# Another order of loads, splits and normalisations in the opening of a two-layer streaming encoder step

## What is computed

```python
c_kv = rmsnorm(kv_lat, lp['mla_kv_norm'])
k_rope = apply_rope(kr_raw, pos)
lat_all = jnp.concatenate([past[0], c_kv], axis=1)      # 512 cached latents of 256, then the new ones
kr_all = jnp.concatenate([past[1], k_rope], axis=1)
kv = (lat_all @ w_kvup).reshape(B, K, MLA_HEADS, MLA_NOPE_DIM + MLA_V_DIM)
k_nope, v = kv[..., :MLA_NOPE_DIM], kv[..., MLA_NOPE_DIM:]
k = rmsnorm(jnp.concatenate([k_nope, kr], axis=-1), qk_k_norm)
```

## Time and profile before

| what | value |
|---|---|
| median of 3 runs | 1045.93 us (1045.85 to 1046.44) |
| profiled execution, its own time | 1047.23 us |
| its span, first to last instruction | 1045.3 us |
| mean granted TensorE clock | 0.998 |
| TensorE busy | 1038.8 us of the span |
| TensorE's share of the chain that ended last | 97% |
| memory read | 142.11 MB, 139 GB/s over the span |

### The profile page before, as it was taken

The page is one execution under the profiler, slowest core; times in us unless marked ns, Lnnn a source line. Parts: engine busy times, 40 slices in busy tenths (PEclk is TensorE's granted clock), DMA queues, the critical chain, the costliest instruction groups (busy, mean ns, idle before and its releaser), DMA issues.

```text
span 1045.3 us, 20059 instructions
## 1 busy us (share of the span) xinstructions
PE 1038.8 (99%) x7586; PEld 1005.6 (96%) x7586; DVE 641.6 (61%) x1079; ACT 506.8 (48%) x930; POOL 314.3 (30%) x277
## 2 busy tenths in 40 slices
PE   8999999999999999999999999999999999999998
PEld 6899999999999999999998999999999999999998
DVE  6888764445766666543567886554557565565443
ACT  6557755444554444434355585554445444433341
POOL 3365566541221111100133755656312211111000
PEclk9999999999999999999999999999999999999999
DMA  7455533244535544454514544333344354444441
GB/s 243 118 157 124 185 103 120 90 133 142 161 120 164 159 146 155 142 180 145 178 45 137 149 145 135 96 119 122 120 154 152 124 177 141 154 147 146 156 145 67
DMA packets 48707, 146.29 MB, mean 140 GB/s; under 512 B 8800, under 2 KB 14400, under 8 KB 48640
## 3 DMA queue, kind: packets, MB, share of 16 engines
q1 hardware_dynamic: 42416, 143.05, 44.3%
q10 hardware_dynamic: 6224, 2.30, 0.9%
HBM read 142.11 MB, written 3.22 MB: 139 GB/s over the span
## 4 chain that ended last, share of the span: by engine, by line
PE 97%; DVE 2%; DMA 0%; ACT 0%; issue 0%; SPq 0%; ACTq 0%
PE psum L566 29%; PE psum L567 28%; PE psum L568 28%; PE psum L739 1%; PE psum L778 1%; PE psum L761 1%; PE psum L721 1%; PE psum L722 1%; PE psum L726 1%; PE psum L769 1%; PE psum L698 1%; PE psum L811 1%; PE psum L994 0%; PE psum L866 0%; PE psum L693 0%; PE psum L694 0%
## 5 line engine op out<-in xcount | busy, mean ns | idle before, releaser
L566 PE MATMUL psum<-AH,WH 128*128 128x320 f32 x1328 | 414.4, 312 | 0.2
L568 PE MATMUL psum<-AH,WL 128*128 128x320 f32 x1328 | 410.3, 309 | 0.0
L567 PE MATMUL psum<-AL,WH 128*128 128x320 f32 x1328 | 410.2, 309 | 0.0
L566 PEld LDWEIGHTS psum<-AH,WH 128*128 128x128 f32 x1328 | 249.3, 188 | 7.3 <-issue 5.5
L567 PEld LDWEIGHTS psum<-AL,WH 128*128 128x128 f32 x1328 | 249.4, 188 | 0.2
L568 PEld LDWEIGHTS psum<-AH,WL 128*128 128x128 f32 x1328 | 249.3, 188 | 0.0
L1077 ACT CAST WH<-raw 128x1024 fp32r<-128x1024 f32 x166 | 172.7, 1046 | 129.2 <-PE psum L568 127.7
L1515 DVE TENSOR_TENSOR WL<-raw,WH 128x1024 fp32r<-128x1024 f32 x103 | 127.6, 1240 | 114.0 <-ACT WH L1077 113.6
L1978 POOL TENSOR_TENSOR WL<-raw,WH 128x1024 fp32r<-128x1024 f32 x60 | 147.6, 2478 | 114.7 <-ACT WH L1077 95.5
L1709 DVE TENSOR_TENSOR WL<-raw,WH 128x1024 fp32r<-128x1024 f32 x88 | 107.5, 1222 | 49.5 <-ACT WH L1250 48.2
L1983 POOL TENSOR_TENSOR fab<-fa,fb 128x320 f32<-128x320 f32 x44 | 38.6, 878 | 264.6 <-DVE fb L1714 264.6
(11 more groups left out here) (284 smaller groups left out, 1580.1 us busy)
## 6 DMA issues: line engine op xcount, KB each, us to landing
raw<-w_all SPq DMA_DIRECT2D x264, 512.0 KB, 3.5
y_out<-X SPq DMA_DIRECT2D x8, 160.0 KB, 2.7
X<-x_in SPq DMA_DIRECT2D x2, 320.0 KB, 5.7
X<-x_in SPq DMA_DIRECT2D x1, 640.0 KB, 7.4
lat_out<-ckv ACTq DMA_DIRECT2D x2, 320.0 KB, 2.9
scratch<-brel SPq DMA_DIRECT2D x8, 63.8 KB, 4.3
ckv<-lat_in SPq DMA_DIRECT2D x1, 384.0 KB, 5.5
bias<-scratch SPq DMA_DIRECT2D x8, 48.0 KB, 4.5
```

Source lines behind the costliest of these rows:

```text
L566: mm(out, WH[:, slot, c0:c0 + cols], high, start=first, stop=False)
L567: mm(out, WH[:, slot, c0:c0 + cols], low, start=False, stop=False)
L568: return mm(out, WL[:, slot, c0:c0 + cols], high, start=False, stop=last)
```

## The change

TensorE's list in layer 0 begins with the value rows of block 0 and then the key rows; its waits are per half of a unit. SP issues the value unit first, the key unit second, then latents 128 to 255, the identity, `par`, the two `gains` loads (moved from ScalarE's queue) and latents 256 to 511. ScalarE's queue issues the first 128 latents and `krT`. ScalarE rounds the two units in two halves each, and no longer the first latents: VectorE does that, then its low part, then four half low parts and the low part of latents 128 to 255. The last latents are split in block 0 (ScalarE after `rope_rows`, VectorE after `key_scale(0)`). In layer 0 `norm_chunk` and `norm_low` move back: on ScalarE chunk 0 to block 1, chunk 1 to block 2, chunks 2 and 3 to block 3; on VectorE chunks 0 and 1 behind block 2, chunks 2 and 3 behind block 3. The low part of unit 3 moves from `key_scale(2)` to `key_scale(3)`, GpSimd's halves of unit 2 from blocks 0 and 1 to 1 and 2. The two `kgain` products go behind `key_scale(0)`. The order of layer 1 stays but for those `kgain` products.

```diff
+LATENTS = (((0, 128), (128, 256), (256, PAST)), ((0, 128), (128, PAST)))
+CKV0 = (0, 4)
...
@@ -495,13 +501,15 @@
     @block.sync
     def _(sp):
         lat = lat_in[0:1].rearrange("a p c n -> (a p) c n")
-        sp.dma_start(ckv[:, :, T:T + 128], lat[:, :, 0:128]).then_inc(s.cache_lat[0], 16)
-        sp.dma_start(raw[:, 0, :], w_all[stored(0)]).then_inc(raw_ready[0], 16)
-        sp.dma_start(raw[:, 1, :], w_all[stored(1)]).then_inc(raw_ready[1], 16)
+        sp.dma_start(raw[:, U_KVV, :], w_all[stored(U_KVV)]).then_inc(raw_ready[U_KVV], 16)
+        sp.dma_start(raw[:, U_KVK, :], w_all[stored(U_KVK)]).then_inc(raw_ready[U_KVK], 16)
+        sp.dma_start(ckv[:, :, T + 128:T + 256], lat[:, :, 128:256]).then_inc(s.cache_lat[1], 16)
         sp.dma_start(cst[:, K_ID:K_ID + 128], cst_in[:, K_ID:K_ID + 128]).then_inc(s.id_in, 16)
-        sp.dma_start(krT[64:96, T:NKEY], kr_in[0:1].rearrange("a p n -> (a p) n")).then_inc(s.cache_kr, 16)
-        sp.dma_start(ckv[:, :, T + 128:NKEY], lat[:, :, 128:PAST]).then_inc(s.cache_lat[1], 16)
         sp.dma_start(par[:, 0:DEPTH * NPAR], par_in).then_inc(s.par_in, 16)
+        gain_pairs = par_in.rearrange("p (l c) -> p l c", c=NPAR)[:, :, C_GQ:C_GQ + 2]
+        for row, at_row in ((96, 80), (112, 64)):
+            sp.dma_start(gains[row:row + 16], gain_pairs[at_row:at_row + 16]).then_inc(s.gains_in, 16)
+        sp.dma_start(ckv[:, :, T + 256:NKEY], lat[:, :, 256:PAST]).then_inc(s.cache_lat[2], 16)
         sp.dma_start(X[:, 0:2, :], x_in[:, 0:2, :]).then_inc(s.x_in[0], 16)
         sp.dma_start(raw[:, 2, :], w_all[stored(2)]).then_inc(raw_ready[2], 16)
         sp.dma_start(X[:, 2:4, :], x_in[:, 2:4, :]).then_inc(s.x_in[1], 16)
@@ -668,17 +676,20 @@
...
+            if kb == 2:
+                pe.wait_ge(s.ckv_ready, CKV0[l] + len(LATENTS[l]))
...
             for c in range(2):
+                if l == kb == 0:
+                    pe.wait_ge(s.high_ready if c else s.first_high, 2 if c else 3)
                 mm(out, ckvH[:, c, keys], wh[:, c], start=c == 0, stop=False)
                 mm(out, ckvL[:, c, keys], wh[:, c], start=False, stop=False)
-            if kb == 0:
+            if kb == 0 and l > 0:
                 pe.wait_ge(s.split_ready, l * NU + U_KVK + 1)
             for c in range(2):
+                if l == kb == 0:
+                    pe.wait_ge(s.split_ready if c else s.first_low, 2 if c else 3)
                 last = mm(out, ckvH[:, c, keys], wl[:, c], start=False, stop=c == 1)
             last.then_inc(s.kn_full, 1)
...
             for c in range(2):
+                if l == kb == 0:
+                    pe.wait_ge(s.first_high, 1 + c)
                 mm(out, ckvH[:, c, keys], WKH[:, U_KVV, c * 512:c * 512 + 512], start=c == 0, stop=False)
                 mm(out, ckvL[:, c, keys], WKH[:, U_KVV, c * 512:c * 512 + 512], start=False, stop=False)
-            if kb == 0:
+            if kb == 0 and l > 0:
                 pe.wait_ge(s.split_ready, l * NU + U_KVV + 1)
             for c in range(2):
+                if l == kb == 0:
+                    pe.wait_ge(s.first_low, 1 + c)
@@ -902,8 +924,12 @@
         for l in range(DEPTH):
 
             for kb in range(CACHED):
-                key_rows(l, kb)
-                value_rows(l, kb)
+                if l == kb == 0:
+                    value_rows(l, kb)
+                    key_rows(l, kb)
+                else:
+                    key_rows(l, kb)
+                    value_rows(l, kb)
                 if kb == 0:
                     turn_rope(l, 0)
                 else:
         def cached_high(l, part):
 
-            keys = (slice(T, T + 128), slice(T + 128, NKEY))[part]
+            keys = slice(*(T + c for c in LATENTS[l][part]))
             act.wait_ge(s.cache_lat[part], 16 * l + 16)
             nc.scalar.copy(ckvH[:, :, keys], ckv[:, :, keys]).then_inc(s.ckv_cache_high, 1)
 
@@ -1254,39 +1280,49 @@
                     act.wait_ge(s.tile_free, l * NT + j * 4 + (T_FFN + 2 * p + 1))
                     A(fth[:, p, :], fa[:, p, :], ACT.Tanh, scale=0.5).then_inc(s.th_ready, 1)
 
+        act.dma_start(ckv[:, :, T:T + 128], lat_in[0:1].rearrange("a p c n -> (a p) c n")[:, :, 0:128]) \
+            .then_inc(s.cache_lat[0], 16)
+        act.dma_start(krT[64:96, T:NKEY], kr_in[0:1].rearrange("a p n -> (a p) n")).then_inc(s.cache_kr, 16)
         act.wait_ge(s.warm_zero, 1)
         A(small[:, 31:32], ssum[:, 0:1], ACT.Sqrt)
-        cached_high(0, 0)
-        gain_pairs = par_in.rearrange("p (l c) -> p l c", c=NPAR)[:, :, C_GQ:C_GQ + 2]
-        for row, at_row in ((96, 80), (112, 64)):
-            act.dma_start(gains[row:row + 16], gain_pairs[at_row:at_row + 16]).then_inc(s.gains_in, 16)
-        high(0, U_KVK)
-        high(0, U_KVV)
+        act.wait_ge(raw_ready[U_KVV], 16)
+        for c in range(2):
+            half = slice(512 * c, 512 * c + 512)
+            nc.scalar.copy(WKH[:, U_KVV, half], raw[:, U_KVV, half]).then_inc(s.first_high, 1)
+        act.wait_ge(raw_ready[U_KVK], 16)
+        for c in range(2):
+            kh, kr = (w.rearrange("k (p c n) -> k c p n", p=4, c=2)[:, c] for w in (WKH[:, U_KVK, :], raw[:, U_KVK, :]))
+            nc.scalar.copy(kh, kr).then_inc(s.high_ready if c else s.first_high, 2 if c else 1)
+        cached_high(0, 1)
 
         for l in range(DEPTH):
             if l > 0:
                 for k in range(4, KC):
                     norm_chunk(l, 0, k, square=False)
             for kb in range(CACHED):
-                key_square(l, kb)
-                if l == 0 and kb == 0:
-                    cached_high(0, 1)
-                elif l == 0 and kb < 3:
-                    high(l, U_KV + kb - 1)
-                value_copy(l, kb)
+                if l == kb == 0:
+                    value_copy(l, kb)
+                    key_square(l, kb)
+                else:
+                    key_square(l, kb)
+                    if l == 0 and kb < 3:
+                        high(l, U_KV + kb - 1)
+                    value_copy(l, kb)
                 if kb == 0:
                     rope_rows(l, 0)
                     if l == 0:
-                        act.wait_ge(s.par_in, 16)
-                        act.wait_ge(s.x_in[0], 16)
-                        norm_chunk(l, 0, 0, square=False)
+                        cached_high(0, 2)
                 key_root(l, kb)
                 if kb > 0:
                     key_columns(l, kb - 1)
                 if l == 0:
                     if kb == 1:
+                        act.wait_ge(s.par_in, 16)
+                        act.wait_ge(s.x_in[0], 16)
+                        norm_chunk(l, 0, 0, square=False)
+                    elif kb == 2:
                         norm_chunk(l, 0, 1, square=False)
-                    elif kb == 2:
+                    elif kb == 3:
                         act.wait_ge(s.x_in[1], 16)
                         norm_chunk(l, 0, 2, square=False)
                         norm_chunk(l, 0, 3, square=False)
@@ -1564,7 +1603,7 @@
                 .then_inc(s.k_ssq, 1)
             if kb in (0, CACHED):
                 rope_mean(l, 0 if kb == 0 else 1)
-            if l == 0 and kb == 2:
+            if l == 0 and kb == 3:
                 dve.wait_ge(s.split_ready, U_KV + 1)
                 low(l, U_KV + 1)
             if kb == KB - 1:
@@ -1722,28 +1761,43 @@
             v.memset(blk[rows, 64 * h:64 * h + 64], 1.0).then_inc(s.flat_made, 1)
             v.memset(blk[rows, 64 - 64 * h:128 - 64 * h], 0.0).then_inc(s.flat_made, 1)
         v.memset(par[:, DEPTH * NPAR:(DEPTH + 1) * NPAR], 0.0).then_inc(s.x_ready, KC)
+        dve.wait_ge(s.cache_lat[0], 16)
+        v.tensor_copy(ckvH[:, :, T:T + 128], ckv[:, :, T:T + 128]).then_inc(s.first_lat, 1)
         cached_low(0, 0)
-        low(0, U_KVK)
-        low(0, U_KVV)
+        for c in range(2):
+            half = slice(512 * c, 512 * c + 512)
+            dve.wait_ge(s.first_high, 1 + c)
+            TT(WKL[:, U_KVV, half], raw[:, U_KVV, half], WKH[:, U_KVV, half].bitcast(F32), ALU.subtract) \
+                .then_inc(s.first_low, 1)
+        for c in range(2):
+            kl, kr, kh = (w.rearrange("k (p c n) -> k c p n", p=4, c=2)[:, c]
+                          for w in (WKL[:, U_KVK, :], raw[:, U_KVK, :], WKH[:, U_KVK, :]))
+            dve.wait_ge(s.high_ready if c else s.first_high, 2 if c else 3)
+            if c == 1:
+                dve.wait_ge(s.first_low, 2)
+            TT(kl, kr, kh.bitcast(F32), ALU.subtract).then_inc(s.split_ready if c else s.first_low, 2 if c else 1)
         cached_low(0, 1)
 
         for l in range(DEPTH):
             step[0] = 0
-            dve.wait_ge(s.par_in, 16)
-            TT(kgain[0:QK], col(C_GK, l, slice(0, QK)), col(C_GQ, l, slice(0, QK)), ALU.mult)
             for kb in range(CACHED):
                 key_scale(l, kb)
+                if l == kb == 0:
+                    cached_low(0, 2)
                 if kb == 0:
+                    dve.wait_ge(s.par_in, 16)
```

(18 more changed lines are left out.)

26 lines of the change are left out of this document (18 added, 8 removed).

## The result

| | median | range | runs |
|---|---|---|---|
| before | 1046.41 us | 1045.85 to 1047.89 | 22 |
| after | 1048.35 us | 1046.76 to 1051.06 | 22 |

The ratio is 1.0018, with a 95% interval of 1.0012 to 1.0023: the change costs 1.9 us, and 1048.35 lies above the forecast range (1043.7 to 1047.5). The profiled execution of after took 1050.09 us, with a span of 1048.3.

What follows compares the result with a forecast made beforehand. TensorE, busy 1038.8 of 1045.3 us, was taken as the bound. The opening wins 2.4 us, VectorE's order leaves 0.1 to 0.9; 0.4 was taken, 1045.93 - 0.4 = 1045.5 us, range 1043.7 to 1047.5.

Steps and rivals of the forecast that it cites:

- the base: Sum made on the profiled execution, 1047.23 us, 1.3 above the median 1045.93; a gain taken off span, own time and median alike.
- won up to here: Opening up to the first dense tile: it starts at 21.4 instead of 23.82, 2.4 us won.
- The ledger: VectorE's work up to chunk 3's low part, ending at 24.3; chunk 3 read at 24.35 to 25.15, gain 0.9 to 0.1.
- rival 1: The new wait of 1.5 to 2.4 us at 22.3 lowers TensorE's clock, costing 1.7: 1047.2; chance 0.20.
- Arrival: First loads: 0.75 us sooner by the second queue, 0.3 cost for the latents; value unit lands at 5.5, latents at 4.4.
- Block 0 and the opening: First product at 6.15, block 0 ends 2.3 us sooner at 9.4: 1.6 from the clock, 0.7 from waits and arrival.
- SP's two `gains` loads: SP's queue in the opening: about 1 us of issue, said to hide in the queue.
- VectorE's order: Low parts for the dense tile come late; TensorE waits on `AL`, and of 2.4 us won 0.9 are left.
- the upper case: Chunk 0's low part takes 0.6 longer beside GpSimd's half, latents' up to 0.15 more; chunk 3 read at 25.15, gain 0.1.
- Rival 4: The clock falls both in the opening and at the wait at 22.3: 1048.6; chance 0.05.
- Behind the dense tiles: GpSimd's sums of squares end 1.1 us ahead of `stat_mix`; the rest moves with the dense tiles, cost 0.

Runs made afterwards that it cites:

- e5: The kernel before with five warm-up products instead of four; 1046.11 us, ratio 0.9998 to before.
- e1: The changed kernel with five unread products put ahead of TensorE's wait for chunk 2 of the first dense tile; 1047.19 us, ratio 1.0014 to before.
- e2: The changed kernel with the two gains loads issued on ScalarE's queue instead of SP's; 1047.17 us, ratio 1.0009 to before.
- e12: e9 with the change's orders of norm_chunk, norm_low, unit 3's low part and GpSimd's halves; 1048.01 us, ratio 1.0013 to before.
- e4: The kernel before, old opening, with only the change's orders of norm_chunk, norm_low, unit 3's low part and GpSimd's halves; 1049.57 us, ratio 1.0031.
- e10: e9 with the first latents issued first on SP's queue, ahead of the value unit, instead of on ScalarE's; 1045.23 us, ratio 0.9992 to before.
- e11: e9 with the two gains loads back on SP's queue, behind par; 1044.95 us, ratio 0.9988 to before.
- e9: e6 with VectorE's two kgain products moved ahead of the first scaling of the keys; 1044.88 us, ratio 0.9985 to before.
- e3: The changed kernel with before's orders of norm_chunk, norm_low, unit 3's low part and GpSimd's halves, new opening kept; 1046.40 us, ratio 1.0001.
- e6: e2 with unit 3's low part and GpSimd's halves as before, chunks 0 and 1 in block 1, 2 and 3 in block 2; 1046.55 us, ratio 1.0000.
- e7: The kernel before, unchanged, run once more for a profile; 1046.97 us, one run.

## Why the prediction was wrong, point by point

*Two steps failed: the base, and the clock behind the wait.* The forecast missed by 1048.35 - 1045.5 = 2.85 us.

*The base, 1.05 us, and the sign.* The prediction saw that the profiled execution was 1.3 us above the median, and took a gain "off all three alike". But the low stretch of the earlier trace rows is what made it longer by 1.0 (1047.20 against 1046.18), and 24 of 28, 27 of 27 and 39 of 41 further runs don't have it. Of the 2.4 us "won up to here" 1.0 wasn't there to be won: the dense tile of e5 starts at 22.83 and not at 23.82. With the typical base the working gives nearly the right answer. A run of 1046.2 has a span of 1044.3, so that `stat_mix` starts at 1044.3 - 1011.1 = 33.2 (33.23 in e5) and chunk 3 is read 8.99 us earlier, at 24.2. The prediction had chunk 3 read in the changed kernel between 24.35 and 25.15; these times count the new opening with the clock kept. Against 24.2 they mean 0.15 to 0.95 slower, where the prediction said 0.1 to 0.9 faster, and after, with the clock kept, is 0.85 slower. The ledger was right and was compared with the wrong clock time.

*The clock behind the wait, 1.3 us: rival 1, given 0.20, and nothing in the forecast.* The fall came in 16 of 22 runs, and e1 shows that TensorE's idle time in the wait brings it. Its price was put at 1.7 and is 1.35 here (1.39 in e2, 1.63 in e12). The argument against it, 22 us of work without a gap in front, was worth nothing: e4, e2 and e12 fall after 1.7 to 1.9 us of wait, with all the same work ahead. The Trainium skill, "TensorE: Matmul & The Clock Gate", section "Part 1: The HAM clock gate", says that the chip watches activity in windows that run free of the kernel, so that the same program changes its clock at different points in different runs. The table agrees: the same kernel falls or doesn't. Since a prediction needs the median, a wait of this size should have been given the fall with a chance of one half or more. Without the fall the time, 1047.06, would have lain within the range, though not on the side of before that was forecast.

*The rest, 0.5 us.* 0.3 is the median of three runs on which the sum was made (1045.93, where 90 runs give 1046.2), and 0.2 is the choice within the ledger's range (0.65 slower on the typical base; 0.85 measured).

*Arrival: somewhat sooner than said.* The value unit was rounded from 4.41 (landed by 5.5, it said), the first product came at 5.66 (6.15), the latents at 4.80 (4.4), so that they and not the unit came last. The 0.75 us counted for the second queue was 0.35 of time (e10).

*Block 0 and the opening: right.* The warm-up now runs into the first product without a gap, the windows show 1.00 from 8.5 to 11.6, block 0 ends at 8.97 (9.4), block 1 begins at 9.33 (9.8), the transposes of block 0 come at 12.45 (12.7), the dense tile at 21.28 (21.4).

*SP's two `gains` loads: right in the time.* They took SP 1.27 us and left a hole in the stream; ScalarE waited 0.54 and 0.69 us for units 2 and 3 in the profiled execution of after, though not in e1's. "This hides in the queue" was said without looking at how many bytes the queue had in hand so early. The price is 0.07 in e11, where nothing is late, and 0.18 at most with the wait there (e2), which the runs can't tell from nothing.

*VectorE's order: right, at the upper end.* The only new wait is on `AL`, as forecast. In the profile it is 2.67 us and not 1.5 to 2.4, and the idle time ahead of block 2's reciprocal is 1.73 instead of 1.0, because unit 3 came late; in e1, e2 and e12 that idle time is 0.93, 0.94 and 0.93, and e1 reads chunk 3 at 24.64, inside the 24.35 to 25.15 of the ledger; the clock-kept median of after puts it at 34.1 - 8.99 = 25.1. The low parts of chunks 0 and 1 took 1.66 together beside GpSimd's half, the upper case (0.55 and 0.55 + 0.6): the row with the longer duration was the one in which GpSimd ran. The prediction leaned to that end and could have gone all the way.

*Rival 4* (both low stretches, 1048.6) has nearly the measured time by luck: the opening's stretch was absent in after's windows as in most of before.

*Behind the dense tiles: right.* GpSimd's sums of squares end ahead of `stat_mix` in every run (in e9 by the least, 31.38 against 31.95); the time from there to the end is constant to 0.15 us (1011.07 to 1011.22).

## What to carry to other kernels

Check that the profiled execution is a typical one before building on a feature of it: a low clock stretch in one profile may be in few of the runs, and then removing it gains nothing. The same holds for the profiles of the change and of each experiment; five of the thirteen read here after the first (after, e3, e6, e7, e12) lay 0.7 to 2.0 us above the median of like executions. When a stage is pulled forward, write down in absolute times when each later engine is done, and move the work that the next stage reads first (here the low parts of the first chunks) forward with it; e9 does that and gains what the change was after. When an order changes, look also at the smallest two-input operation of VectorE beside a long one of GpSimd: it can cost as much as the long one lasts.
